# Later transposes, an earlier division and interleaved output projections in a five-block transformer kernel

## The reference

```
first block, for layer in (0, 1):
    h = rms_norm(x) * (1 + scale) + shift              # scale, shift, gate: six vectors per layer, silu(c) @ ada_w + b
    y = attention(h) @ w_o  if layer == 0  else  retention(h) @ ret_w_o      # retention output is 2048 wide
    x = x + gate * y
    h = rms_norm(x) * (1 + scale) + shift
    x = x + gate * ((silu(h @ w_gate) * (h @ w_up)) @ w_down)
second block, for layer in (0, 1) (the "hybrid" layers):
    proj = rmsnorm(x) @ w_in
    y_a  = a gated three-tap convolution
    y_b  = eight heads of causal attention (MLA): q and k come from two low-rank parts c_q, c_kv
           (each with its own rmsnorm) and a rotary key k_pe, are normed per head, then rotated
    y_c  = eight heads of dilated attention in three groups (dilation 1, 4, 16): one softmax over
           the scores of all three groups, o = sum over groups of p_g @ v_g
    merged = sum of sigmoid(gate) * (y @ w_out) over a, b, c
    x = x + merged @ w_o
```

## Time and profile before

| | |
|---|---|
| median of 3 runs | 1548.32 us (1542.97 to 1555.18) |
| the profiled execution | 1547.82 us |
| its span, first to last instruction | 1545.8 us |
| mean granted TensorE clock | 0.99 |
| PE busy | 1488.8 us (96%) |
| DVE, ACT busy | 1040.0 us (67%), 857.8 us (55%) |
| DMA | 292.63 MB, 189 GB/s in the mean |

### The profile page before, as it was taken

The page is one execution under the profiler, slowest core; times in us unless marked ns, Lnnn a source line. Parts: engine busy times, 40 slices in busy tenths (PEclk is TensorE's granted clock), DMA queues, the critical chain, the costliest instruction groups (busy, mean ns, idle before and its releaser), DMA issues.

```text
span 1545.8 us, 30529 instructions
## 1 busy us (share of the span) xinstructions
PE 1488.8 (96%) x11764; PEld 1397.6 (90%) x11764; DVE 1040.0 (67%) x1821; ACT 857.8 (55%) x1454; POOL 87.9 (6%) x136
## 2 busy tenths in 40 slices
PE   8988999999999999999999999899999999989999
PEld 7777999999989999999998988789999898878998
DVE  2787788899954556555667666776676765676664
ACT  3445666544455646565566765555556675555453
POOL 0110000111000000000020000310000000031000
PEclk9999999999999999999999999999999999999999
DMA  9776488898754355666663554136666356413663
GB/s 374 270 243 200 136 294 291 289 370 324 266 188 127 115 158 171 192 190 193 196 214 113 162 179 134 56 96 193 192 192 197 120 160 179 126 55 98 199 194 124
DMA packets 81327, 292.63 MB, mean 189 GB/s; under 512 B 9201, under 2 KB 10481, under 8 KB 81089
## 3 DMA queue, kind: packets, MB, share of 16 engines
q1 hardware_dynamic: 67408, 244.03, 49.3%
q0 software_dynamic: 11792, 42.83, 8.2%
q10 hardware_dynamic: 2016, 4.21, 0.8%
HBM read 289.99 MB, written 1.05 MB: 188 GB/s over the span
## 4 chain that ended last, share of the span: by engine, by line
PE 49%; issue 38%; DVE 6%; ACT 3%; POOL 3%; DMA 1%; ACTq 0%; SPq 0%; POOLq 0%; DVEq 0%
PE G L465 13%; PE G L466 13%; PE G L467 13%; POOL bias L441 2%; DVE wlo L1449 2%; PE G L493 1%; PE G L491 1%; PE G L492 1%; DVE aw L1457 1%; PE G L513 1%; ACT whi L1001 1%; PE Tp L775 1%; PE G L519 1%; PE Tp L574 0%; DMA rows<-in_rows 0%
## 5 line engine op out<-in xcount | busy, mean ns | idle before, releaser
L1449 DVE TENSOR_TENSOR wlo<-raw,whi 128x1024 fp32r<-128x1024 f32 x444 | 542.9, 1225 | 306.6 <-ACT whi L1001 304.0
L465 PE MATMUL G<-h,whi 128*128 128x256 f32 x2096 | 599.2, 286 | 5.3 <-DVE cz L1992 3.5
L1001 ACT ACTIVATE whi<-raw 128x1024 fp32r<-128x1024 f32 x444 | 469.0, 1058 | 238.3 <-PE G L467 187.2
L466 PE MATMUL G<-h,whi 128*128 128x256 f32 x2096 | 584.5, 279 | 0.0
L467 PE MATMUL G<-h,wlo 128*128 128x256 f32 x2096 | 584.3, 279 | 0.0
L465 PEld LDWEIGHTS G<-h,whi 128*128 128x128 f32 x2096 | 398.3, 190 | 15.0 <-issue 8.0
L466 PEld LDWEIGHTS G<-h,whi 128*128 128x128 f32 x2096 | 397.9, 190 | 1.7 <-issue 0.5
L467 PEld LDWEIGHTS G<-h,wlo 128*128 128x128 f32 x2096 | 397.4, 190 | 0.0
L1457 DVE CUSTOM_DVE_ANT_0 aw<-aw,cs,cols 128x1024 f32<-128x1024 f32 x80 | 102.3, 1278 | 0.0
L465 PE MATMUL G<-ah,whi 128*128 128x256 f32 x352 | 97.2, 276 | 0.0
L466 PE MATMUL G<-ah,whi 128*128 128x256 f32 x352 | 97.2, 276 | 0.0
(11 more groups left out here) (324 smaller groups left out, 2312.5 us busy)
## 6 DMA issues: line engine op xcount, KB each, us to landing
raw<-in_w SPq DMA_DIRECT2D x444, 512.0 KB, 3.7
aw<-in_ada POOLq DMA_DIRECT2D x80, 512.0 KB, 5.3
adaw<-in_ada SPq DMA_DIRECT2D x8, 1024.0 KB, 17.6
sn<-in_uq ACTq DMA_DIRECT2D x2, 768.0 KB, 4.2
x<-in_x SPq DMA_DIRECT2D x1, 1024.0 KB, 5.6
pt<-in_ukv ACTq DMA_DIRECT2D x2, 512.0 KB, 5.4
out<-x SPq DMA_DIRECT2D x4, 256.0 KB, 2.1
dist<-in_dist POOLq DMA_DIRECT2D x1, 576.0 KB, 6.0
```

Of the source, the lines that this page charges most:

```text
L465: pe.matmul(o, wh, mv[:, 0:T], start=(k == 0), stop=False)
L466: pe.matmul(o, wh, mv[:, T:2 * T], start=False, stop=False)
L1001: act.activation(whi[:, s, :], raw[:, s, :], ACT.Copy).then_inc(w_hi, 1)
L1449: dve.tensor_tensor(wlo[:, s, :], raw[:, s, :], whi[:, s, :], ALU.subtract).then_inc(w_lo, 1)
```

## The change

1. `BESIDE`: attention step 9 gets two weight blocks instead of one, the blocks behind them come one step earlier, step 16 is left with one instead of two.
2. The third group's transposition of a dilated head leaves its own step on PE and goes between the two parts of the next head's scores (head 14: ahead of the block of step 16; head 15 keeps all three together).
3. `normalise(i)` stands at the end of DVE's step i instead of behind the minima of step i+1.
4. Both kinds of output projection named above use `run_late`: the first two tiles are made in turns, first the early pieces of both (12 of 16, 6 of 8), then the late ones of both.
5. `keep_busy` between the two matmuls of `sum_of_squares` goes from 4 to 2.
6. The turning of k_pe moves from j = 1 to 2, and everything of the MLA chain from `mla_projections` up to the second rotation comes one j later. `mla_transposes` stays at 16.
7. Modulation dots 68 to 79 move from retention blocks 1 to 12 to blocks 17 to 28.

```diff
-    BESIDE[0 if _n < 3 else _n - 2 if _n < 18 else 16].append(H_CZ + _n)
+    BESIDE[0 if _n < 3 else _n - 2 if _n < 12 else _n - 3].append(H_CZ + _n)
...
+            def run_late(b, g, k_of, early, moving, each_k, b4=0, g4=0):
+                for m in range(2):
+                    pe.wait_ge(slot_free[(g + m - 2) % 4], taken(g + m - 2) + g4)
+                ended, told = set(), 0
+                for m, ks in ((0, range(early)), (1, range(early)), (0, range(early, k_of)), (1, range(early, k_of))):
+                    o = gslot(g + m)
+                    for k in ks:
+                        n, c = (m * k_of + k) // 8, k % 8
+                        slot = (b + n) % 4
+                        if c == 0:
+                            pe.wait_ge(w_lo, b + n + 1 + 4 * b4)
+                        if m == 0:
+                            each_k(k)
+                        mv = moving(m, k)
...
+                        if c == 7:
+                            ended.add(n)
+                            new = 0
+                            while told in ended:
+                                told, new = told + 1, new + 1
+                            if new:
+                                ins.then_inc(blk_done, new)
+                n = 2 * k_of // 8
+                run(b + n, g + 2, 6, k_of, moving, b4=b4, g4=g4)
...
-                keep_busy(4, S[:, 0, :])
+                keep_busy(2, S[:, 0, :])
...
+            run_late(B_RET_O, G_RET_O, 16, 12, lambda m, k: yr[:, k, :], lambda k: pe.wait_ge(r_lo, k // 4 + 1))
...
+                    if j == 2:
+                        rotary_key()
+                    if j == 4:
                         mla_projections()
...
+                    for part, units in enumerate((((3 * p + 2 * e, 0), (3 * p + 2 * e, 64)), ((3 * p + 1, 64 * e),))):
+                        if part:
+                            between()
...
+                def third_group(i):
+                    if i > 8:
+                        to_keys(sn[:, (i - 1) % 2, 2, :], 3)
...
+                        dil_scores(i - 8, lambda: third_group(i - 1))
+                    elif i == 16:
+                        third_group(15)
...
-                        for grp in range(1 if i <= 8 else 3):
+                        for grp in range(1 if i <= 8 else 3 if i == 16 else 2):
...
+                run_late(B_HYB + H_WO, G_HYB + HYB_TILES - 8, 8, 6, lambda m, k: mh[:, k, :],
+                         lambda k: pe.wait_ge(m_lo, l * 8 + k + 1), b4, g4)
...
-                if 1 <= b <= 12:
-                    ada_later(67 + b)
+                if 17 <= b <= 28:
+                    ada_later(51 + b)
...
-                    if j in (12, 14):
+                    if j in (13, 15):
                         mla_rope(j // 2 - 6)
...
-                    if 1 <= i <= 16:
-                        normalise(i - 1)
...
+                    if i < 16:
+                        normalise(i)
```

More of the change, by code:

```diff
@@ L473, in run @@
                 assert t % 8 == 0
+            def run_late(b, g, k_of, early, moving, each_k, b4=0, g4=0):
[12 more added lines that the diff above has]
+                        mv = moving(m, k)
+                        wh, wl = whi[:, slot, c * P:(c + 1) * P], wlo[:, slot, c * P:(c + 1) * P]
+                        pe.matmul(o, wh, mv[:, 0:T], start=(k == 0), stop=False)
+                        pe.matmul(o, wh, mv[:, T:2 * T], start=False, stop=False)
+                        ins = pe.matmul(o, wl, mv[:, 0:T], start=False, stop=(k == k_of - 1))
+                        if c == 7:
[7 more added lines that the diff above has]
+                run(b + n, g + 2, 6, k_of, moving, b4=b4, g4=g4)
             def run_tokens(b, g, j, b4=0, g4=0):
@@ L795, in _ @@
             ret_sum(4, r_sq, 4)
-            run(B_RET_O, G_RET_O, 8, 16, lambda m, k: yr[:, k, :],
-                each_k=lambda k: pe.wait_ge(r_lo, k // 4 + 1))
+            run_late(B_RET_O, G_RET_O, 16, 12, lambda m, k: yr[:, k, :], lambda k: pe.wait_ge(r_lo, k // 4 + 1))
             sum_of_squares(3)
@@ L857, in lora_sums, with rotary_key @@
                         ins.then_inc(t_done, 1)
+                def rotary_key():
                     slot = use_t()
@@ L906, in _ @@
                         lora_sums()
-                    if j == 3:
+                    if j == 2:
+                        rotary_key()
+                    if j == 4:
                         mla_projections()
@@ L920, in mla_scores, with dil_scores @@
                     pe.matmul(S[:, slot, P:384], q[:, P:T], kk, start=True, stop=True).then_inc(s_done, 1)
-                def dil_scores(head):
+                def dil_scores(head, between):
                     p, e = head // 2, head % 2
-                    for units in (((3 * p + 2 * e, 0), (3 * p + 2 * e, 64)), ((3 * p + 1, 64 * e),)):
+                    for part, units in enumerate((((3 * p + 2 * e, 0), (3 * p + 2 * e, 64)), ((3 * p + 1, 64 * e),))):
+                        if part:
+                            between()
                         slots = [use_s() for _ in units]
@@ L963, in _ @@
                     elif i < 16:
-                        dil_scores(i - 8)
+                        dil_scores(i - 8, lambda: third_group(i - 1))
+                    elif i == 16:
+                        third_group(15)
                     if i >= 3 and i % 2:
@@ L986, in _ @@
                             half=half_done)
-                run(B_HYB + H_WO, G_HYB + H_MERGE + 48, 8, 8, lambda m, k: mh[:, k, :], b4=b4, g4=g4,
-                    each_k=lambda k: pe.wait_ge(m_lo, l * 8 + k + 1))
+                run_late(B_HYB + H_WO, G_HYB + HYB_TILES - 8, 8, 6, lambda m, k: mh[:, k, :],
+                         lambda k: pe.wait_ge(m_lo, l * 8 + k + 1), b4, g4)
         @block.scalar
@@ L1339, in _ @@
                         lora_roots()
-                    if j == 4:
+                    if j == 2:
+                        rotary_key()
+                    if j == 5:
                         act.wait_ge(qk_in, l + 1)
                         act.activation(qks[:, :, :, :], qk[:, :, :, :], ACT.Square).then_inc(qk_sq, 1)
-                    if j == 7:
+                    if j == 8:
                         act.wait_ge(qk_ss, l + 1)
@@ L1870, in mla_in @@
                         dve.tensor_copy(vm[:, tt, :], S[:, slot, :]).then_inc(s_free, 1)
-                    dve.wait_ge(t_free, L1_T + l * HYB_T + 4)
+                    dve.wait_ge(t_free, L1_T + l * HYB_T + 5)
                     for tt in range(2):
@@ L1927, in _ @@
                         lora_gain()
-                    if j == 3:
+                    if j == 4:
                         mla_in()
-                    if j == 6:
+                    if j == 7:
                         mla_sums()
-                    if j == 9:
+                    if j == 10:
                         mla_scale()
-                    if j == 10:
+                    if j == 11:
                         dve.wait_ge(in_hyb, 64)
                         mla_gain()
-                    if j in (12, 14):
+                    if j in (13, 15):
                         mla_rope(j // 2 - 6)
```

## The result

The changed kernel takes 1541.7 us (median of 20 runs, 1530.6 to 1549.5) against 1550.2 for the kernel before (20 runs, 1543.0 to 1557.0): a ratio of 0.9936, 95% interval 0.9918 to 0.9954. By this ratio the gain is 9.9 us (7.1 to 12.7) where 20.6 were forecast, and the time is 1.7 us outside the range. The forecast counted from 1548.3, the median of 3 runs of the kernel before, and the median of 20 stands 1.9 above that. The profiled execution took 1540.8 us.

A forecast was written before the change was run, and what follows sets the result against it. TensorE, busy 96% of the span, was taken as the bound. 1547.8 - 18.4 - 4.5 - 1.8 - 1.3 - 1.1 + 3.5 + 3.0 = 1527.2, with the median 0.5 higher: 1528 us, range 1519 to 1540.

The forecast's parts named there:

- 1, attention: Attention of the two hybrid layers: waits and clock loss fall from 16.9 to 7.7 us a layer, gaining 18.4 us.
- 2, retention projection: Retention output projection: the 2.8 us wait for `yr` and the 1.7 us clock drop behind it go, gaining 4.5 us.
- 2, hybrid projection: Hybrid output projections: a wait of 0.9 us, twice, hides under a cover of 2.1, gaining 1.8 us.
- 3, fillers: Sums of squares at three places: two fewer fillers start the second matmul 0.44 us sooner, gaining 1.3 us.
- 4, dots: Retention block 8: without the dot ahead of the rotation, the 1.2 us wait for `wlo` goes, gaining 1.1 us.
- 5, MLA chain with its clock: Hybrid layers: transposes wait 3.4 us for the later chain, costing 3.5 us in all plus 3.0 for clock drops.
- one drop in every second case: Attention: half clock follows the remaining long waits in half the cases, costing 0.9 us per layer.
- the sum of the laying out: Attention: measured durations laid end to end in the new queue order give 6.8 us of waits per layer.
- Rival (a): Attention: waits are moved, not removed; gain 5 us a layer, time 1537; chance 0.23.
- Rival (b): Attention: the division at the step's end becomes a serial chain and the kernel gets slower, 1580; chance 0.04.
- a sum of 1533: Sums of squares: fewer fillers could bring a 3.4 us clock drop at three places, costing 5; left out of the forecast.
- Rival (c): Hybrid layers: the wait at the MLA transposes does not come because the chain ends early enough, 1521; chance 0.11.

The follow-up runs named there:

- fifth run: The kernel before with only the three attention edits (block order, third transposition, division): 1537.4 us, ratio 0.9886.
- sixth run: The changed kernel, but the second tile of the projections in turns asks for its PSUM slot only when it begins: 1535.3 us, ratio 0.9879.
- third run: The kernel before with two fillers instead of four, nothing else: 1556.8 us, ratio 1.0006.
- fourth run: The changed kernel with MLA transposes one step later and the second tile's slot asked for when that tile begins: 1524.2 us, ratio 0.9801.
- the same, first: The changed kernel run again, nothing altered: 1536.8 us, 0.989 of the kernel before.
- four fillers, second: The changed kernel with four fillers again in each sum of squares: 1538.7 us, 0.9915 of the kernel before.
- tenth: The same kernel as in the fourth run, measured again on another chip: 1524.2 us, ratio 0.9818.
- MLA chain back, seventh: The changed kernel with the MLA chain where it was before: 1532.6 us, 0.985 of the kernel before.
- block order back, eighth: The changed kernel with the attention weight blocks as before, one in step 9 and two in step 16: 1533.1 us, ratio 0.9851.
- both mends and block order, ninth: The kernel of the fourth run with the attention weight blocks ordered as before the change: 1523.5 us, ratio 0.983.

## Why the prediction was right or wrong

The stages give what each step is worth: the pair of profiled executions, and for half clock the share of all traces in which a wait was followed by it.

| step, us gained | forecast | stages |
|---|---|---|
| 1, attention | +18.4 | +17.4 |
| 2, retention projection | +4.5 | +4.5 |
| 2, hybrid projection | +1.8 | **-1.4** |
| 3, fillers | +1.3 | +1.3 |
| 4, dots | +1.1 | +1.1 |
| 5, MLA chain with its clock | -6.5 | -6.5 |
| sum | +20.6 | +16.4 |

**Attention: the mechanism was right, one term too small, and in part luck.** Steps 0 to 7 gained 2.4 and 2.3. Steps 8 to 16 take 77.6 before, 71.6 after with a half-clock stretch behind the step-10 wait and 70.1 without. The prediction put "one drop in every second case"; it stands in 12 of 16 layers of the traces with this block order. 2 x (2.35 + 7.5 - 0.75 x 1.5) = 17.4. At one in two it would be 18.2, so the sum of the laying out holds within 0.2. Its terms do less well. The waits by starts: step 1 1.2 (forecast 1.1), step 9 0.9 (1.2), **step 10 1.7 (2.2)**, and the third transposition of head 14 in step 16 about 0.4 (1.3). It starts 1.14 behind the first of three transpositions, where two of them take 0.75 at the end of step 14:

```profile
1018.14 0.82 PE L852 MATMUL Tp<-ident,sn 128*128 128x128 f32 x6
1018.89 0.93 PE L963 MATMUL S<-dqk 64*128 64x128 f32 x8
...
1026.11 0.82 PE L852 MATMUL Tp<-ident,sn 128*128 128x128 f32 x6
1027.25 0.55 PE L852 MATMUL Tp<-ident,sn 128*128 128x128 f32 x3 [0.32 <-ACT pt L1455]
```

The four terms together are 1.6 less than forecast, and yet the gain is no larger, so something else in the stage cost about as much; no row here says what. Rival (a), that the waits are moved and not removed, falls with the fifth run: 17.4 by stages, 17.7 (11.5 to 24.0) by the runs, against the 10 that it left. Its time, 1528 + 8.4, is 1536 and not 1537. The measured 1541.7 lies nearer to it than to the forecast, but not for its reason. Rival (b) falls with the list of waits: nothing waits for the division.

**Retention projection: right.** 48.51 - 43.97 = 4.54, no wait for `yr`, PEclk 1.00 over 541 to 550. Both of these ran at the fast pace; at the slow one it is 49.84 (fifth run) - 45.56 = 4.3.

**Hybrid projection: this step failed.** The prediction gave "1.8" for two waits of 0.9 against a cover of 2.1, and asked who reads the second tile's slot early in the retention projection, but not here, where it put the wait for that slot at nothing. In the retention projection ScalarE has long read it, and no wait stands at its head; here VectorE reads it, behind a low of 1.23. The head of the projection costs 1.41 a layer and the projection itself gives back 0.78 and 0.64: 2.82 - 1.42 = 1.4 lost. In the other four traces with the early question it gives back less, 0.3 to 0.4 in the first layer and 0.2 to 0.8 in the second, and the loss is 1.7 to 2.3. The sixth run takes out the 2.8 by moving one wait, and what is left of the step there is a gain of 1.4 against the forecast 1.8.

**Fillers: right.** 0.45, 0.45 and 0.39. By the Trainium skill ("TensorE: Matmul & The Clock Gate", Part 1) throttled is the default state and activity releases the clock, from which I had a sum of 1533 with a stretch at each of the three places. The traces do not bear that sum out: none of the nine with two fillers has a half-clock stretch behind a norm, and the mean clock with two and with four fillers is 0.9930 and 0.9928. The third run alone, -0.9 (-5.9 to 4.2), could not have shown 1.3; the stages do.

**Dots: right.** The blocks gain 1.69 and the token part gives 0.59 back: 1.1. That is one pair; the mean of the three traces with the dots early less that of the nine with them late is 0.9, and no run moves the dots alone.

**MLA chain: right.** The stage from the low-rank sums takes 1.98 and 1.89 more (forecast 1.7 each), the wait is 3.32 (3.4), and a stretch at half clock, 27.25 - 25.62 = 1.6, stands behind it in 8 of 10 layers of the traces that have this wait: 1.3 a layer (1.5). Together 6.5. Rival (c), that the wait does not come, falls. The chain can go later without loss if its end goes with it, which the fourth run shows: the transposes' stages gain 7.1, the token blocks give 0.9 back and the low-rank stages 3.9, 2.3 gained instead of 6.5 lost.

**From 16.4 to 9.9.** Are the stage sums what a median shows? Gains worked out as (1 - ratio) times the median before, in us, beside what the stages give for each kernel:

| kernel | stages | measured (interval) |
|---|---|---|
| the changed kernel, 20 runs | 16.4 | 9.9 (7.1 to 12.7) |
| the same, first | 16.4 | 17.1 (10.9 to 23.3) |
| four fillers, second | 15.1 | 13.2 (8.4 to 17.9) |
| fillers alone, third | 1.3 | -0.9 (-5.9 to 4.2) |
| two mends, fourth and tenth | 28.0 | 30.9 (24.1 to 37.6), 28.2 (23.9 to 32.7) |
| part 1 alone, fifth | 17.4 | 17.7 (11.5 to 24.0) |
| slot late, sixth | 19.2 | 18.8 (12.6 to 24.9) |
| MLA chain back, seventh | 22.9 | 23.3 (15.6 to 31.1) |
| block order back, eighth | 17.8 | 23.2 (17.1 to 29.2) |
| both mends and block order, ninth | 29.4 | 26.4 (20.9 to 31.6) |

Ten of the eleven intervals hold the stage sum, though they are 9 to 16 us wide; the first row does not, though it is the same kernel as the second. What makes up its missing 4 to 9 us **stays open**. In the profiled pair the untouched stages account for it with 9.4 us, and that execution is within 1 us of the median of its 20, but what the other 19 held is not known. The two paces are a candidate: runs of the changed kernel with the same mean clock, 0.992, go from 1539.2 to 1549.4 us, and one slow feed-forward is 4.5 + 2.3 = 6.8. Only profiled executions show the pace, so the 20 runs can't be sorted by it. The forecast had no term for it, and took the kernel's spread of 0.8% for a matter of the measurement. Of the 10.7 us by which the gain fell short, 3.2 are a wrong step (the hybrid projection, 1.8 forecast and -1.4 measured), 1.0 a mis-sized one (half clock in the attention, in three cases of four instead of every second one), and 6.5 are not attributed. That most terms came out does not make it a good forecast of the time: untouched stages took back 9.4 us in the profiled execution, and it had no term for them.

## What to carry to other kernels

Before a chain is moved later, look at how long its end lies ahead of its consumer: a chain that already ended 0.2 us late had no slack for a step of 3.2, so the consumer moves along or the whole step is paid. When a reordering gathers waits at one place, ask of each buffer who reads it last and what stands ahead of that reader; moving one wait to the tile that needs it took 2.8 us of waits away here. For changes under 1% compare the starts of the same instructions in several traces, stage by stage, and leave out the stages that no edit touches: they differed by up to 7 us here.

## What the hardware did that I had not expected

The stream of matmuls with a weight load each has two paces at full granted clock, 851 and 885 in 100 us. One of them can hold over a whole feed-forward, a projection or a merge, and it can also change from block to block. I saw no wait, clock or DMA share that goes with the one or the other ahead of the stretch, and its cause is open. In the attention steps it is not all chance: in each of the 20 layers with the attention's edits, the blocks of steps 13 and 15 go through at 0.1175 us per matmul and those of steps 12 and 14 at 0.1135, while in the four layers without the edits either pace stands in steps 12, 13 and 15. The same wait can be followed by a stretch at half clock or not: the 1.7 us of step 10 in 12 layers of 16, the 3.3 us at L916 in 8 of 10.
